# Shifting the activations by 64 bytes against the weights in a two-block transformer kernel

## The reference

```python
# first block, for each of two layers
x = x + jnp.concatenate([mix, cross], axis=-1) @ w_o[i]
x = x + squared_relu_mlp(rmsnorm(x, mlp_norm_g[i]), mlp_w_up[i], mlp_w_down[i])
# second block, for each of two layers
x = x + g_m[:, None, :] * (mixed @ w_out)
hf = modulate(rms_norm(x, ffn_norm), sh_f, sc_f)
return x + g_f[:, None, :] * swiglu(hf, ffn_w_gate, ffn_w_up, ffn_w_down)
```

## Time and profile before

| | before |
|---|---|
| runs (us) | 1219.35, 1213.15, 1218.85 |
| median of the runs | 1218.85 |
| the profiled execution's own time | 1212.2 |
| its span, first to last instruction | 1210.6 |
| mean granted TensorE clock | 0.997 of full |
| TensorE matmuls | 9675, busy 98% of the span |
| read from memory | 247.79 MB, 206 GB/s over the span |

### The profile page before, as it was taken

The page is one execution under the profiler, slowest core; times in us unless marked ns, Lnnn a source line. Parts: engine busy times, 40 slices in busy tenths (PEclk is TensorE's granted clock), DMA queues, the critical chain, the costliest instruction groups (busy, mean ns, idle before and its releaser), DMA issues.

```text
span 1210.6 us, 23530 instructions
## 1 busy us (share of the span) xinstructions
PE 1189.6 (98%) x9675; PEld 1155.0 (95%) x9675; DVE 871.5 (72%) x1159; ACT 647.7 (54%) x873; POOL 117.2 (10%) x178
## 2 busy tenths in 40 slices
PE   8999999999999999999999999999999999999998
PEld 8998999999998999999999999999988779999998
DVE  5765797777776697877889988886576557855443
ACT  7557566634337566643468463443455675544332
POOL 0000011111115011011110001110000150000000
PEclk9999999999999999999999999999999999999999
DMA  9452488787862388787764557876645404466452
GB/s 332 158 174 71 143 276 299 262 292 273 278 234 100 109 275 292 265 312 282 262 214 157 158 176 255 285 267 224 221 152 198 150 1 140 150 210 196 143 195 79
DMA packets 150011, 250.00 MB, mean 207 GB/s; under 512 B 5505, under 2 KB 80618, under 8 KB 149930
## 3 DMA queue, kind: packets, MB, share of 16 engines
q1 hardware_dynamic: 135810, 198.21, 48.4%
q0 software_dynamic: 13952, 50.60, 11.6%
q10 hardware_dynamic: 168, 0.04, 0.0%
HBM read 247.79 MB, written 1.05 MB: 206 GB/s over the span
## 4 chain that ended last, share of the span: by engine, by line
PE 89%; DVE 6%; ACT 2%; issue 1%; POOL 0%; DMA 0%; DVEq 0%; POOLq 0%; ACTq 0%
PE ps L2126 26%; PE ps L2127 26%; PE ps L2128 26%; DVE w_lo L1255 3%; PE ps L2394 2%; PE ps L2264 1%; PE ps L2376 1%; PE ps L2180 1%; PE ps L2213 1%; DVE scratch L1729 1%; PE ps L2363 1%; PE ps L2689 0%; PE ps L2652 0%; PE ps L2207 0%; POOL sb_u L631 0%
## 5 line engine op out<-in xcount | busy, mean ns | idle before, releaser
L1255 DVE TENSOR_TENSOR w_lo<-raw,w_hi 128x2048 fp32r<-128x2048 f32 (+4 forms) x196 | 412.7, 2144 | 102.5 <-ACT w_hi L744 102.2
L744 ACT ACTIVATE w_hi<-raw 128x2048 fp32r<-128x2048 f32 (+4 forms) x196 | 342.4, 1792 | 166.6 <-PE ps L2128 166.6
L2126 PE MATMUL ps<-h_both,w_hi 128*128 128x256 f32 (+1 forms) x1296 | 362.5, 280 | 2.5 <-ACT cqT L865 1.0
L2128 PE MATMUL ps<-h_both,w_lo 128*128 128x256 f32 (+1 forms) x1296 | 360.1, 278 | 0.0
L2127 PE MATMUL ps<-h_both,w_hi 128*128 128x256 f32 (+1 forms) x1296 | 360.1, 278 | 0.0
L2126 PEld LDWEIGHTS ps<-h_both,w_hi 128*128 128x128 f32 (+1 forms) x1296 | 243.0, 188 | 3.8 <-issue 3.3
L2127 PEld LDWEIGHTS ps<-h_both,w_hi 128*128 128x128 f32 (+1 forms) x1296 | 243.8, 188 | 0.1
L2128 PEld LDWEIGHTS ps<-h_both,w_lo 128*128 128x128 f32 (+1 forms) x1296 | 243.1, 188 | 0.0
L2126 PE MATMUL ps<-a_both,w_hi 128*128 128x256 f32 x864 | 240.8, 279 | 0.0
L2127 PE MATMUL ps<-a_both,w_hi 128*128 128x256 f32 x864 | 240.1, 278 | 0.0
L2128 PE MATMUL ps<-a_both,w_lo 128*128 128x256 f32 x864 | 240.0, 278 | 0.0
(11 more groups left out here) (426 smaller groups left out, 1894.8 us busy)
## 6 DMA issues: line engine op xcount, KB each, us to landing
ada_raw<-in_l_ada_w POOLq DMA_DIRECT2D x96, 512.0 KB, 6.6
raw<-in_mlp_w_up SPq DMA_DIRECT2D x32, 1024.0 KB, 6.5
raw<-in_mlp_w_down SPq DMA_DIRECT2D x32, 1024.0 KB, 6.4
raw<-in_l_ffn_w_gate SPq DMA_DIRECT2D x22, 1024.0 KB, 5.4
raw<-in_l_ffn_w_up SPq DMA_DIRECT2D x22, 1024.0 KB, 7.9
raw<-in_l_ffn_w_down SPq DMA_DIRECT2D x16, 768.0 KB, 5.7
raw<-in_l_w_qkv SPq DMA_DIRECT2D x12, 1024.0 KB, 7.0
raw<-in_l_w_in SPq DMA_DIRECT2D x10, 1024.0 KB, 6.6
```

Of the source, the lines that this page charges most:

```text
L744: nc.scalar.activation(w_hi[:, s.slot, cut], raw[:, s.slot, cut], ACT.Copy).then_inc(split_hi, 1)
L1255: nc.vector.tensor_tensor(w_lo[:, s.slot, cut], raw[:, s.slot, cut], w_hi[:, s.slot, cut].bitcast(F32), ALU.subtract).then_inc(split_lo, 1)
L2126: nc.tensor.matmul(to, sh, mh, start=first, stop=False, skip_group_check=True)
L2128: return nc.tensor.matmul(to, sl, mh, start=False, stop=last, skip_group_check=True)
```

## The change

`line_h` grows from 48 to 64 float32 on each partition, from 192 to 256 bytes. No instruction is added, removed or moved on any engine.

```diff
-        sb("line_h", [P, 48])
+        sb("line_h", [P, 64])
         h_wide = sb("h_wide", [P, 2, KD, T + 2], F32R)
```

## The result

The changed kernel takes 1242.32 us in the median of four runs (1241.11 to 1242.97). The kernel before, run beside it, takes 1219.1 (1213.15 to 1222.27). The ratio is 1.0215, with a 95% interval from 1.0173 to 1.0257: slower by some 2%, with the interval reaching to both sides of 2%. The profiled execution took 1241.11 us, against 1212.2 before, 28.9 us more.

A forecast was written before the change was run, and what follows sets the result against it. TensorE's matmul count times step was taken to bound the kernel; 28.1 + 5.2 + 0.4 + 1.9 + 0.8 = +36.4 us on 1212.2 gave 1248.6, stated as 1248 us, range 1216 to 1257.

The forecast's parts named there:

- What bounds the kernel: TensorE, busy 98% of the span: time is its matmul count times the start-to-start step; only the step can move.
- 256 behaves as 0: At distance 256 every 256-column product steps at 120.0 ns, as `keep_warm` does at distance 0.
- (a): 256-column matmuls now at 113.3 ns go to 120.0: 4220 x 6.7 ns = +28.1 us.
- (b): 256-column matmuls now at 117.8 ns go to 120.0: 2350 x 2.2 ns = +5.2 us.
- (c): `l` remains a mixture, 0; the 192 matmuls of `m` lose 2.2 ns each, +0.4 us.
- (d): 258-column products of `h_wide` and `u`: +1.9 us, bounds 0 and 5.8 us, -1.9 us also possible.
- (e): 378 products: 288 with stationary `h_both`, 90 with `cq` and `ckv`: +0.8 us, bounds 0 and 2.5 us.
- The base: The profiled execution's 1212.2 us, to which the forecast's sum of +36.4 us was added.
- All at the middle level: Rival: 256-column products settle at 117.8 ns, only those at 113.3 lose; +18.8 us, 1231 us, chance 0.20.
- no difference: Rival: distance has no bearing, levels come from how a stream is begun; 1212 to 1219 us, chance 0.13.
- the first level everywhere: Rival: all streams stand at 276 ns and the 2350 slower matmuls gain; -10.5 us, 1202 us, chance 0.12.
- worse than `keep_warm`: Rival: products of 258 and 512 columns lose their full bounds, 5.6 us more; 1254 to 1261 us, chance 0.05.

The follow-up runs named there:

- d128: The kernel before with the `line_h` filler cut to 128 bytes, so split operands lie 128 from the weights: 1235.63 us, ratio 1.012.
- the map: The kernel before plus 74 streams of 24 throwaway matmuls behind the second `keep_warm`, weights past weights at stepped distances, 128 then 32 stationary columns: 1423.54 us.
- all64: The kernel before with a 64-byte filler ahead of the first buffer, moving weights and activations together, distance still 192: 1216.83 us, ratio 0.9988.
- d0: The kernel before with the `line_h` filler taken out, distance 0: 1242.04 us, ratio 1.0189.
- arena256: The kernel before with `line_a` grown by 64 bytes: a, o, l and u go to 256, h stays at 192; 1228.56 us, ratio 1.0106.
- arena144: The kernel before with `line_h` at 128 bytes and each arena buffer 16 bytes into its room (h at 128, arena at 144): 1235.25 us, ratio 1.0135.

## Why the prediction was right

**What bounds the kernel.** Right. Only TensorE's steps moved, and but for 3.4 us of the clock the difference is in them.

**256 behaves as 0.** Right, to the digit: 283 ns and 120.0 ns a step in every long stream, no second level, `keep_warm` unchanged. (Two short streams of 48 matmuls, at 26 and 34 us, average 118.8 and 115.4; the second holds the products with 32 stationary columns.) But the step that led there, "the pattern seems to repeat every 128 bytes", was wrong: the period is 256, by d128 and by the map. The evidence was `u`, where four distances gave the same step. With 258 columns the matmuls never reach the first level, and what the distance does there is small: in the changed kernel the distances of `u` are all others, and its 384 products cost 47.4 us, before 47.5. I read an insensitive shape as a symmetry. And the two stretches of `u` could not have told 128 from 256 in any case: modulo 256 chunks 0 and 1 lie at 192 and 64, and chunks 2 and 3 at 192 and 64 again. The second piece of evidence was no better: I took it from `l` that the part at 256 makes the longest matmul, but with its high part at 256 after the change, all three lines stand at 278 to 279 ns. And `keep_warm` was not the one case at 0: `m_hi` lies there as well, next to `m_lo` at 192. That 256 is alike to 0 follows from the true period as well. The number was right by that, partly by luck, since it stood on a wrong leg.

**(a) and (b).** 33.3 us forecast; `h_both`, `a_both` and `o` together lost 32.9 before rounding.

**(c)** +0.4 forecast, +0.4 measured; `l` stayed at its 22.6 us.

**(d) and (e).** +1.9 and +0.8 forecast, -0.3 and -0.7 measured, inside the bounds for (d), just outside for (e), where I had excluded a gain without a reason. The gain is no chance: the 378 products cost 83.9 us at 256 and at 0, 84.6 before, and 85.8 to 86.0 at 64, 128, 160, 224 and 320. With the activations stationary and 384 or 512 columns of weights streaming, 0 and 256 are the best places and not the worst. Together (d) and (e) were 3.7 us too much.

**The base.** The rest between 36.4 forecast and 28.9 in the profiles is the clock, 3.4 us, which the profiled execution before lost in the heads and the one after did not. I had not looked for it: the page's line shows full clock in each slice, while the mean was 0.997.

**The runs' spread.** I took it that the spread comes from how many streams fall on which level, and goes when there is one level. After the change four runs lie within 1.9 us, and at distance 0 two within 0.6; at distance 192, 15 runs of the kernel before beside each other lie from 1210.92 to 1224.7, and all64 from 1208.38 to 1225.22. The clock has a share in that: its mean was 0.992 to 1.0 in those 15 runs. With the lost clock taken off each run (its time times one less the mean clock), the kernel before still spans 8 us (1207.9 to 1216.1), the changed one 2 (1239.2 to 1241.1). The mean clock is given to 0.001 only, which is 1.2 us. By these numbers the median lost 26 us rather than 23. That the remaining 8 us are the levels is not shown: of the runs only profiled executions can be read by stream, and in three with all these products at 192 (before, all64, map) `h_both`, `a_both` and `o` cost the same within 1.5 us. It fits that the spread goes when there is one level.

**The rivals.** "All at the middle level" is out by 283 ns; "no difference" is out by d0 and arena256; "the first level everywhere" is out with it, and "worse than `keep_warm`" by (d) and (e), which lost nothing. The Trainium skill, "SBUF — State Buffer", section "Who interferes with whom", which says that TensorE's two read ports are independent and that it never waits on anyone, would have had the same step at all distances. The map shows 2.94 to 3.09 us for the same 24 matmuls, with nothing changed but the start of the moving operand, and another pattern with 32 stationary columns; the measurements decide against it for float32r.

## What to carry to other kernels

Where a stream of matmuls bounds a kernel, read the step from start to start by stretch and not as a mean over the run: two levels in one group of lines are a finding. The duration tells levels apart only within one kind of stream: 281 ns goes with 117.8 ns at 192, and in arena144 with 120.0. Then look where stationary and moving operand start modulo 256 bytes; in this kernel, with 128 stationary and 256 streamed float32r columns and the weights in their place, 64, 192 and 320 were best and 0 and 256 worst, at a price of 2% of the whole, and a filler of 64 bytes ahead of a buffer changes it. Measure the real products, since a probe that loads the same weights each time gave the right period, but not the right step at every distance; the two kernels with the weights moved by 16 bytes, built on it, took 1245 us.

## What was not expected

One shape at one distance has two stable steps, 113.3 and 117.8 ns, and keeps the one it fell into for up to 157 us, through 1385 matmuls. There are two at 128 as well (118.7 and 120.0) and at 144 (116.7 and 118.7); the real products at 0 and 256 have one. The period of the effect is 256 bytes to within 0.01 us in 3, at all sixteen places of the map with 128 stationary columns; the real products show it at 0 and 256 and at 64 and 320. And no stream of 256 float32r columns ran faster than 113.3 ns a step. The Trainium skill, "TensorE: Matmul & The Clock Gate", section "Back-to-back issue gap", gives N / 2.4 + 2.5 ns for a matmul by itself, an estimate of 109.2 for 256 columns. By it, even the best placement here leaves 4 ns a matmul. No distance of the map, and not the 32 stationary columns either, came below 113.3.
